# Stick-breaking attention: weights from two sigmoids and a running product, multiplied on GpSimd, in a two-block transformer kernel

## The reference, cut to what matters

```python
def stick_breaking_attention(q, k, v):
    """q, k, v: (B, S, H, dh). A[t,s] = sigmoid(z_ts) * prod_{s<j<t} (1 - sigmoid(z_tj)), s < t only."""
    ...
    def block(i):
        start = i * Q_BLOCK
        q_blk = lax.dynamic_slice_in_dim(qh, start, Q_BLOCK, axis=2)
        z = jnp.einsum('bhqd,bhkd->bhqk', q_blk, kh).astype(jnp.float32) * inv_sqrt
        q_pos = start + jnp.arange(Q_BLOCK)
        mask = key_pos[None, :] < q_pos[:, None]
        log_1m_beta = jnp.where(mask, jax.nn.log_sigmoid(-z), 0.0)
        suffix = lax.cumsum(log_1m_beta, axis=3, reverse=True) - log_1m_beta
        a = jnp.where(mask, jnp.exp(jax.nn.log_sigmoid(z) + suffix), 0.0)
        return jnp.einsum('bhqk,bhkd->bhqd', a, vh.astype(jnp.float32)).astype(q.dtype)
```

## Time and profile before

| | us |
|---|---|
| median of 3 runs | 3073.14 |
| lowest and highest | 3069.12, 3074.96 |
| the profiled execution's own time | 3063.84 |
| its span, first to last instruction | 3062.1 |
| TensorE busy in the span | 2875.2 (94%) |
| attention of the second block, about 1864 to 2104 us of the span | 240 |
| busy in it: TensorE, VectorE, ScalarE, GpSimd | 202.3, 197.3, 139.0, 27.5 |

### The profile page before, as it was taken

One profiled execution on the slowest core, in us unless ns is written; L12 is line 12 of the kernel. 1 busy time (PEld: TensorE's weight loads), 2 busy tenths in 40 slices (PEclk: granted clock), 3 DMA queues, 4 the chain that ended last, 5 costly groups with the idle time before them and its releaser, 6 DMA issues.

```text
span 3062.1 us, 42914 instructions
## 1 busy us (share of the span) xinstructions
PE 2875.2 (94%) x16394; PEld 2321.4 (76%) x16394; DVE 1624.6 (53%) x2005; ACT 752.3 (25%) x1421; POOL 1058.9 (35%) x746
## 2 busy tenths in 40 slices
PE   7998898979899999999799999879998999999997
PEld 6886567868788888888678886657876888888886
DVE  3464544662677777777732005884134455445545
ACT  3323564323311111101420004563124001100111
POOL 4321001348534333333643322112358333323333
PEclk9998999999999999999899999999999999999999
DMA  3200000013222222222221111001131111111111
GB/s 123 55 27 11 10 6 22 3 48 133 69 89 77 81 82 85 87 82 82 83 69 45 51 35 35 15 1 56 55 124 56 55 41 55 48 48 43 53 49 61
DMA packets 213435, 172.12 MB, mean 56 GB/s; under 512 B 15543, under 2 KB 188878, under 8 KB 213326
## 3 DMA queue, kind: packets, MB, share of 16 engines
q1 hardware_dynamic: 160670, 135.47, 14.3%
q10 hardware_dynamic: 52656, 35.13, 3.8%
HBM read 162.19 MB, written 8.39 MB: 56 GB/s over the span
## 4 chain that ended last, share of the span: by engine, by line
PE 82%; DVE 8%; POOL 4%; issue 2%; ACT 2%; DMA 1%; SPq 0%; DVEq 0%; ACTq 0%; POOLq 0%
PE ps L873 13%; PE ps L875 13%; PE ps L874 13%; PE ps L1290 7%; PE ps L1291 7%; PE ps L1292 7%; PE ps L1082 2%; PE ps L1000 2%; DVE sb_weights L2476 1%; PE ps L892 1%; PE ps L894 1%; PE ps L893 1%; POOL rstd L666 1%; PE ps L1022 1%; POOL slab_lo L240 1%
## 5 line engine op out<-in xcount | busy, mean ns | idle before, releaser
L237 POOL TENSOR_SCALAR slab_hi<-raw 128x1024 fp32r<-128x1024 f32 (+1 forms) x236 | 263.4, 1116 | 1540.4 <-PE ps L875 581.1
L240 POOL TENSOR_TENSOR slab_lo<-raw,slab_hi 128x1024 fp32r<-128x1024 f32 (+1 forms) x236 | 576.8, 2444 | 19.7
L873 PE MATMUL ps<-act_hi,slab_hi 128*128 128x512 f32 x1472 | 575.2, 391 | 2.0 <-DVE act_lo L1986 1.6
L875 PE MATMUL ps<-act_hi,slab_lo 128*128 128x512 f32 x1472 | 572.9, 389 | 0.0
L874 PE MATMUL ps<-act_lo,slab_hi 128*128 128x512 f32 x1472 | 572.7, 389 | 0.0
L2391 DVE TENSOR_TENSOR acc<-ps,acc 128x512 f32<-128x512 f32 x512 | 339.5, 686 | 200.6 <-PE ps L1292 200.5
L1290 PE MATMUL ps<-slab_hi,hid_hi 128*128 128x512 f32 x1024 | 403.4, 394 | 4.2 <-POOL acc L794 2.5
L1291 PE MATMUL ps<-slab_hi,hid_lo 128*128 128x512 f32 x1024 | 399.5, 390 | 0.0
L1292 PE MATMUL ps<-slab_lo,hid_hi 128*128 128x512 f32 x1024 | 399.3, 390 | 0.0
L1813 ACT ACTIVATE relu<-ps 128x512 f32<-128x512 f32 x128 | 77.0, 602 | 1041.2 <-PE ps L875 1023.1
L873 PEld LDWEIGHTS ps<-act_hi,slab_hi 128*128 128x128 f32 x1472 | 276.4, 188 | 59.8 <-DVE act_lo L1986 1.7
(11 more groups left out here) (320 smaller groups left out, 4252.9 us busy)
## 6 DMA issues: line engine op xcount, KB each, us to landing
raw<-in_w_in SPq DMA_DIRECT2D x56, 512.0 KB, 3.8
w_ada<-in_w_ada ACTq DMA_DIRECT2D x48, 512.0 KB, 4.1
raw<-in_w_out SPq DMA_DIRECT2D x32, 512.0 KB, 3.4
raw<-in_w_up SPq DMA_DIRECT2D x32, 512.0 KB, 4.1
...
```

The source lines that it names most:

```text
L237: pool.tensor_scalar(self.hi[s][:, 0:width], self.raw[r][:, 0:width], 1.0, 0.0, ALU.mult, ALU.add)\
L240: pool.tensor_tensor(self.lo[s][:, 0:width], self.raw[r][:, 0:width], self.hi[s][:, 0:width].bitcast(F32), ALU.subtract).then_inc(self.spl ...
L873: pe.matmul(o, hi[:, w], a_hi[:, k, cols], start=(k == 0), stop=False)
L875: mm = pe.matmul(o, lo[:, w], a_hi[:, k, cols], start=False, stop=(k == nk - 1))
```

## The change

The logarithms go. With beta = sigmoid(z), the weight of key s is beta_s times the product of (1 - beta_j) over the later keys, and 1 - beta = sigmoid(-z).

- **VectorE** adds the mask constant (0 below the diagonal, -1e30 elsewhere) onto the last 128 columns of the scores in PSUM (`sb_mask`), and makes the running product of `sb_rest` from the last key backwards (`sb_remainders`, the same scan with mult for add). The cap and the subtraction go.
- **ScalarE** reads the scores from PSUM twice: sigmoid(z) into `sb_weights`, sigmoid(-z) into `sb_rest`, of which there are two buffers (`sb_betas`). So the scores' banks come free with the second sigmoid (`sb_beta_done`), and the second sigmoid of item s waits until the product of item s-2 has been multiplied (`sb_arg_done`). The turned blocks are copied out without exp. The table set of the sigmoid is loaded for that of exp and ln.
- **GpSimd** multiplies `sb_weights` by `sb_rest`, shifted by one key (`sb_weights`), for each of the 64 items. Two of its panel splits stand behind items 7 and 11 of the pairs 0, 1 and 3.
- **TensorE** makes the scores of the next tile behind the turn of the same step, not ahead of it.

```diff
-            for i in range(SB_PAIRS):
+            def sb_weights(i, s):
+                n = (s // 2 + 1) * P
+                w = sb_w[s % SB_SLOTS][:, 0:n - 1]
+                pool.wait_ge(sem("sb_rest_done"), SB_ITEMS * i + s + 1)
+                pool.tensor_tensor(w, w, sb_rest[s % 2][:, 1:n], ALU.mult).then_inc(sem("sb_arg_done"), 1)
+
+            for i in range(2):
                 for j in range(2):
                     R8.split(pool, 2 * i, i, j)
-            merge_splits(R9, 0, range(2))
+            for i in range(SB_PAIRS):
+                for s in range(SB_ITEMS):
+                    sb_weights(i, s)
+                    if s in (7, 11) and i + 2 < SB_PAIRS:
+                        R8.split(pool, 2 * (i + 2), i + 2, s // 11)
+                    if s in (7, 11) and i + 1 == SB_PAIRS:
+                        merge_splits(R9, 0, (s // 11,))
...
-                pe.wait_ge(sem("sb_z_copied"), SB_ITEMS * i + 2 * t + 2)
+                pe.wait_ge(sem("sb_beta_done"), SB_ITEMS * i + 2 * t + 2)
...
-                    if s % 2 and s + 1 < SB_ITEMS:
-                        sb_scores(i, s // 2 + 1)
                     if s % 2 == 0 and s < 12 and not last:
                         sb_project(i + 1, s // 3, SB_THIRDS[s % 3])
                     if s % 2 == 0 and (late := lagged(i, before, s, SB_LAG_PV, SB_ITEMS)):
                         sb_outputs(late[0], late[1] // 2)
                     if late := lagged(i, before, s, SB_LAG_TURN, SB_ITEMS):
                         sb_turn(*late)
+                    if s % 2 and s + 1 < SB_ITEMS:
+                        sb_scores(i, s // 2 + 1)
...
-            def sb_softplus(i, s, before):
-                n = (s // 2 + 1) * P
-                z, l = sb_z[s % 2][:, 0:n], sb_w[s % SB_SLOTS][:, 0:n]
-                act.wait_ge(sem("sb_z_copied"), SB_ITEMS * i + s + 3)
+            def sb_betas(i, s, before):
+                n, at = (s // 2 + 1) * P, SB_ITEMS * i + s
+                z = ps[:, 2 * (s % 2):2 * (s % 2) + 2, :].rearrange("p b n -> p (b n)")[:, 0:n]
+                act.wait_ge(sem("sb_masked"), at + 1)
                 if slot := lagged(i, before, s, SB_SLOTS, SB_ITEMS):
                     act.wait_ge(sem("sb_turned"), SB_GROUPS * slot[0] + (sb_groups(slot[1])[-1] + 1))
-                act.activation(l, z, ACT.Exp).then_inc(sem("sb_exp_done"), 1)
-                act.wait_ge(sem("sb_exp_done"), SB_ITEMS * i + s + 1)
-                act.activation(l, l, ACT.Ln, bias=1.0).then_inc(sem("sb_ln_done"), 1)
+                act.activation(sb_w[s % SB_SLOTS][:, 0:n], z, ACT.Sigmoid)
+                if at >= 2:
+                    act.wait_ge(sem("sb_arg_done"), at - 1)
+                act.activation(sb_rest[s % 2][:, 0:n], z, ACT.Sigmoid, scale=-1.0).then_inc(sem("sb_beta_done"), 1)
...
-                    act.activation(sb_at[g % 4][:, 0:w], ps[:, 4 + g % 2, 0:w], ACT.Exp).then_inc(sem("sb_at_done"), 1)
+                    act.copy(sb_at[g % 4][:, 0:w], ps[:, 4 + g % 2, 0:w]).then_inc(sem("sb_at_done"), 1)
...
+            def sb_mask(i, s):
+                f, col = divmod(s // 2 * P, HALF)
+                diagonal = ps[:, 2 * (s % 2) + f, col:col + P]
                 dve.wait_ge(sem("sb_scores"), SB_ITEMS * i + s + 1)
+                dve.tensor_tensor(diagonal, diagonal, consts[:, C_KEYCAP:C_KEYCAP + P], ALU.add).then_inc(sem("sb_masked"), 1)
+
+            def sb_remainders(i, s):
+                n, at = (s // 2 + 1) * P, SB_ITEMS * i + s
+                rest = sb_rest[s % 2]
+                dve.wait_ge(sem("sb_beta_done"), at + 3)
+                dve.tensor_tensor_scan(rest[:, 0:n][:, ::-1], rest[:, 0:n][:, ::-1], rest[:, 0:n][:, ::-1], 1.0, ALU.mult, ALU.bypass)\
+                    .then_inc(sem("sb_rest_done"), 1)
+
+            sb_mask(0, 0)
+            sb_mask(0, 1)
             for i in range(SB_PAIRS):
                 for s in range(SB_ITEMS):
-                    if s + 1 < SB_ITEMS:
-                        sb_cap_scores(i, s + 1)
-                    elif i + 1 < SB_PAIRS:
-                        sb_cap_scores(i + 1, 0)
-                    sb_log_weights(i, s)
+                    sb_remainders(i, s)
+                    if s % 2 == 0:
+                        for h in range(2):
+                            if s + 2 < SB_ITEMS:
+                                sb_mask(i, s + 2 + h)
+                            elif i + 1 < SB_PAIRS:
+                                sb_mask(i + 1, h)
```

More of the change, by code:

```diff
@@ L65 @@
 SB_LAG_TURN, SB_LAG_PV = 2, 4
-SB_Z_CAP = 40.0
+SB_MASKED = -1e30
 def sb_groups(s):
@@ L167, in constants @@
         c[:, C_LEVEL + n * CHUNK:C_LEVEL + (n + 1) * CHUNK] = ((k[:, :CHUNK] // s) % 2 == 1) & (r % CHUNK // s == k[:, :CHUNK] // s - 1)
-    c[:, C_KEYCAP:C_KEYCAP + P] = np.where(k < r, SB_Z_CAP, -1e30)
+    c[:, C_KEYCAP:C_KEYCAP + P] = np.where(k < r, 0.0, SB_MASKED)
     c[:, C_ID64:C_ID64 + CHUNK] = r % CHUNK == k[:, :CHUNK]
@@ L431, in two_blocks @@
         k2 = [sb(f"k2_feat{i}", kb, [P, SEQ]) for i, kb in enumerate((21, 85))]
-        sb_z = [sb(f"sb_z{i}", 41 + 4 * i, [P, SEQ]) for i in range(2)]
+        sb_rest = [sb(f"sb_rest{i}", 41 + 4 * i, [P, SEQ]) for i in range(2)]
         sb_w = [sb(f"sb_weights{i}", kb, [P, SEQ]) for i, kb in enumerate((49, 53, 73, 77))]
@@ L1470, in _ @@
                 sb_pair(i)
-            pe.wait_ge(sem("sb_z_copied"), SB_ITEMS * SB_PAIRS + 2)
+            pe.wait_ge(sem("sb_beta_done"), SB_ITEMS * SB_PAIRS + 2)
             merge_gate(R9, 1, 0, 0)
@@ L1888, in _ @@
                 act.copy(v2[:, t, :, :].rearrange("p h e -> p (h e)"), ps[:, t, :]).then_inc(sem("v2_done"), 1)
[L1891 removed]
+            act.preload_act_table_set("sigmoid_and_others")
             z_scale = float(SB_DIM) ** -0.5
@@ L1930, in sb_pair @@
                         sb_take_projection(i + 1, s // 3 - 1)
-                    sb_softplus(i, s, before)
+                    sb_betas(i, s, before)
                     if late := lagged(i, before, s, SB_LAG_TURN, SB_ITEMS):
@@ L2458, in _ @@
                         .then_inc(sem("m_done"), 1)
-            key_cap = consts[:, C_KEYCAP:C_KEYCAP + P]
-            def sb_cap_scores(i, s):
-                n = (s // 2 + 1) * P
-                z, scores = sb_z[s % 2], ps[:, 2 * (s % 2):2 * (s % 2) + 2, :].rearrange("p b n -> p (b n)")
+            def sb_mask(i, s):
+                f, col = divmod(s // 2 * P, HALF)
+                diagonal = ps[:, 2 * (s % 2) + f, col:col + P]
                 dve.wait_ge(sem("sb_scores"), SB_ITEMS * i + s + 1)
-                if n > P:
-                    dve.tensor_scalar(z[:, 0:n - P], scores[:, 0:n - P], SB_Z_CAP, None, ALU.min)
-                dve.tensor_tensor(z[:, n - P:n], scores[:, n - P:n], key_cap, ALU.min).then_inc(sem("sb_z_copied"), 1)
@@ L2472, in sb_log_weights @@
-            def sb_log_weights(i, s):
-                n = (s // 2 + 1) * P
-                z, l = sb_z[s % 2][:, 0:n], sb_w[s % SB_SLOTS][:, 0:n]
-                dve.wait_ge(sem("sb_ln_done"), SB_ITEMS * i + s + 1)
-                ch.link(dve.tensor_tensor_scan(l[:, ::-1], l[:, ::-1], l[:, ::-1], 0.0, ALU.add, ALU.bypass))
-                dve.wait_ge(sem("sb_z_copied"), SB_ITEMS * i + s + 3)
-                dve.tensor_tensor(l, z, l, ALU.subtract).then_inc(sem("sb_arg_done"), 1)
-                dve.wait_ge(sem("sb_arg_done"), SB_ITEMS * i + s + 1)
```

4 lines of the change are left out of this document (1 added, 3 removed).

## The result

The changed kernel takes 3109.95 us (median of 4 runs, 3106.94 to 3110.45), the kernel before 3072.68 beside it (3069.12 to 3074.96): ratio 1.0127, 95% interval 1.0113 to 1.0141. It is slower by 37 us. The forecast was 3103, range 3070 to 3134.

A forecast was written before the change was run, and what follows sets the result against it. TensorE was taken to bound the narrow tiles, VectorE the wide tiles and last pair. Terms 19.5 + 3.3 + 7.1 = 29.9 us onto 3063.8 give 3093.7; with the median 9.3 above, 3103, range 3070 to 3134.

The forecast's parts named there:

- The largest term: Tiles 1 to 6, three pairs: TensorE waits for ScalarE's second sigmoid to free scores' banks; 6.5 us a pair, 19.5 together.
- the 0.4 for a projection's copy: At items 3 and 9 a projection's copy stands in ScalarE's queue too and adds 0.4 us each to TensorE's stall.
- The step that failed: Narrow tiles: the 6.5 us stall a pair counts in full, as TensorE is the bound and nothing else can absorb it.
- The rival on the clock: New stalls drop TensorE's clock: two more half-speed spells of 2 us in each of four pairs, 16 us, 3119; chance 0.14.
- the wide tiles: Tiles 6, 7 and 0: the new chain gives 25.3 us against 24.2, +1.1 a pair, 3.3 in three pairs.
- the chain: Last pair: mask, two scans, multiply, sigmoid, scores and handoffs set the pace; 47.6 us against 40.5, +7.1.
- The 0.4 for five handoffs: Estimated 0.4 us for the five handoffs between engines, between the ends of two tiles' scores in the new chain.
- scan and multiply exclude each other: VectorE's scan and GpSimd's multiply wait for each other whole; scans at 1024 take 2.3 us first, up to 4.7 behind.
- The rival's order, multiply first: GpSimd gets the port before the second scan, one scan leaves the chain: 9 us off, 3094; chance 0.20.
- the splits: GpSimd's splits between multiplies, about 3.5 us each: taken as zero cost; without cover six would cost up to 6 us.
- The sum: Whole kernel: 19.5 + 3.3 + 7.1 = 29.9 us onto the profiled 3063.8, so 3093.7; median forecast 3103.
- the waits' terms, 5.6 and 0.8: Narrow tiles, a pair: 5.6 us of stalls for t = 1 to 5, plus 0.4 each for projection copies at two items.

The follow-up runs named there:

- e1: Against the changed kernel, ScalarE copies the turned blocks one item later (item s-3, not s-2); ratio to the kernel before 1.0090.
- e3: Against the changed kernel, ScalarE's copies one item later and TensorE's scores ahead of the turn; ratio to the kernel before 1.0066.
- e4: Against the changed kernel, VectorE multiplies behind each scan and GpSimd has only its splits; ratio to the kernel before 1.0049.
- e5: Against the changed kernel, GpSimd multiplies only the first 127 columns of each item, the rest stays unmultiplied; ratio to the kernel before 1.0068.

## Why the prediction was right, point by point

**Right: the cause and the place.** The largest term, TensorE waiting for scores' banks in tiles 1 to 6 of three pairs, is what the trace shows. The five waits were forecast at 6.5 us a pair and are 6.3. Tile by tile, with the 0.4 for a projection's copy, they were forecast at 1.1, 0.9, 1.1, 1.75 and 1.55 and are 1.30, 1.02, 1.32, 1.93 and 0.76: the first four are 0.1 to 0.2 too low, and the last is half, since there TensorE has already waited 0.66 us ahead of the turn before. e1 and e3 show the cause, copies queued ahead of sigmoids.

**Mis-sized: the narrow stretch as a whole.** I forecast 6.5 us a pair on top, 19.5 in three, and it was 28.0. The step that failed is the one that set the loss equal to these waits. Of the 9.1 us in pair 2, 6.3 are the waits, 0.7 is a wait that I didn't have (the second turn of tile 4 waits for a bank that ScalarE's copies free) and 1.6 the half clock; 0.5, which is busy time of TensorE and no wait, is left unexplained. The rival on the clock had this mechanism, with 16 us in all; measured are 4.9 in the narrow stretches of pairs 0 to 2, and 3 to 5 by estimate in the last pair. The spells were more than I had there, but one costs only what is on the path in it. The Trainium skill, "TensorE: Matmul & The Clock Gate", section "HAM oscillation — how this bites in real kernels", has it that waits that come back make the kernel restart at half clock each time. The trace agrees in part: the last pair is at 0.81, with waits of 2.1, 3.3, 3.5 and 4.0 us ahead of the second turns of tiles 3 to 6, but behind the wait of 3.31 us the turn and tile 6's scores ran at full clock (0.76 and 1.77 us, rows at 2104.33 and 2105.18 above), while those of tiles 3 and 4 ran at half behind waits of 1.15 us at most.

**Right but small: the wide tiles.** Forecast +1.1 us a pair, 3.3 in all; measured +0.4, +2.0 and -1.1, together +1.3. The stretches also differ in granted clock (1.00, 0.87 and 0.93 after; 0.93, 0.93 and 0.86 before), so the single values say little about the chain.

**The last pair: the chain is right, the sum by luck.** Forecast 47.6 us, measured 48.05. Tile by tile the chain was forecast at 4.5, 4.7, 5.9, 7.0, 8.1, 9.2 and 8.2, and is 4.2, 4.6, 6.0, 7.8, 7.8, 10.0 and 7.8. In four of these the scores themselves ran at half clock: those of tiles 3, 4, 5 and 7 took 2.08, 2.51, 2.93 and 3.46 us, 5.0 more in all than at full. Without that the chain is 43.1, so two errors cancel: the clock, which the sum didn't have, and a chain that was 4.5 too long. Of this the multiply is 1.5: I had it at 2.39 us for 1024 columns, as the add, where it takes 2.00. The other 3.0 aren't taken apart; at 256 and 384 columns the multiply went first, and a scan fell out of the chain. The 0.4 for five handoffs was my estimate; in the rows above the multiply was issued 0.07 us after its scan's end (2119.49) and the sigmoid 0.03 after the multiply's (2123.23).

**Right: scan and multiply exclude each other; mostly the scan goes first.** In the last pair, from 512 to 896 columns, both scans ran and then the multiply, as the sum had it. The rival's order, multiply first, came at 256 and 384 columns, and at 1024, where a scan took 3.01 us, and 3.30 at the longest in all pairs (I had said up to 4.7). The Trainium skill, "SBUF — State Buffer", section "Who interferes with whom", describes it as an exclusive lock that goes to whoever issued first; the rows at 2117.37 and 2119.56 above agree: the first scan ended at 2119.49, the second, queued behind it, had started at 2119.41, and the multiply, issued at 2119.56, got next to nothing until that had ended. What the port costs by itself wasn't isolated. e4 takes it away together with the longer duration, the handoffs to GpSimd and the half clock, and gets 14 us in the last pair and 1.5 in the wide stretch; e5 shortens the duration, and most of the half clock goes with it (only tile 7's scores have it, 3.46 us); it gets 8 and 2.

**Open: the splits.** I took zero. In the last pair (splits at 2095.43 and 2112.41) the turns behind them didn't wait, but the scan of 640 columns beside the multiply that the first had delayed took 1.91 us, against 1.48 in e4. The wide stretches of pairs 0 and 1, with splits, are 24.3 and 25.8, that of pair 2 without them 23.1. That difference isn't theirs alone: e4 has no splits between multiplies, and its three are 23.1, 23.1 and 21.6. No kernel moved the splits alone.

**The sum.** Forecast +29.9 on the profiled execution, measured 37.8 in the attention. The missing 7.9 are +8.5 in the narrow stretches, -2.0 in the wide ones, +0.5 in the last pair up to the merge panel and +0.9 behind it, where the merge's first 2.3 us ran at a granted clock of 0.56 (1.00 before). By the medians the loss is 37.3. Two slips in the working changed little: the waits' terms, 5.6 and 0.8, add up to 6.4 and not 6.5, and pair 0's narrow stretch was 32.9 us before, not 35.7.
